# SyncE takes over the wait for the last landings, and GpSimd gets a drain of its own ahead of the four late gathers

## What is computed

```
x = x + concat(y_s5, y_lru) @ w_out
x = x + cross_attend(x, mem_k, mem_v)
gate_w    = softmax(top2(le of the best group)) * pg_sel          # top 2 of 8 experts in the best of 4 groups
combine   = sum_k one_hot(expert_id[k], 32) * gate_w[k]
act       = silu(hf @ w_gate[e]) * (hf @ w_up[e])
out       = sum_e (act * combine[e]) @ w_down[e]
y_prompt, y_sample = rmsnorm(x + out, g_final)
```

## Time and profile before

| | us |
|---|---|
| median of three runs | 1136.78 (1136.31 to 1136.99) |
| the profiled execution | 1137.67 |
| its span | 1135.9 |
| PE busy | 1079.8 |
| DVE busy | 697.8 |
| ACT busy | 277.6 |
| POOL busy (221 instructions) | 191.3 |

### The profile page before, as it was taken

One profiled execution on the slowest core, in us unless ns is written; L12 is line 12 of the kernel. 1 busy time (PEld: TensorE's weight loads), 2 busy tenths in 40 slices (PEclk: granted clock), 3 DMA queues, 4 the chain that ended last, 5 costly groups with the idle time before them and its releaser, 6 DMA issues.

```text
span 1135.9 us, 15543 instructions
## 1 busy us (share of the span) xinstructions
PE 1079.8 (95%) x6141; PEld 617.8 (54%) x6141; DVE 697.8 (61%) x1352; ACT 277.6 (24%) x570; POOL 191.3 (17%) x221
## 2 busy tenths in 40 slices
PE   6999999999999999999999999999899999999991
PEld 4666766678765444788867645555633333333330
DVE  4576499927866655743266677776643555455455
ACT  5201321256652111100033311111301222222232
POOL 5000010101000000000000000000122454565554
PEclk9999999999999999999999999999799999999996
DMA  9109460178373201400045451015789999999951
GB/s 300 42 1 211 41 42 1 45 214 290 122 306 116 65 1 55 168 1 1 1 185 199 172 183 65 32 56 204 284 285 378 412 411 413 414 415 411 411 199 66
DMA packets 75244, 204.97 MB, mean 180 GB/s; under 512 B 25480, under 2 KB 34336, under 8 KB 66816
## 3 DMA queue, kind: packets, MB, share of 16 engines
q1 hardware_dynamic: 54336, 168.82, 42.3%
q0 software_dynamic: 20704, 35.09, 9.1%
q10 hardware_dynamic: 128, 0.03, 0.0%
HBM read 195.23 MB, written 52.18 MB: 218 GB/s over the span
## 4 chain that ended last, share of the span: by engine, by line
PE 80%; DMA 8%; DVE 5%; issue 4%; POOL 1%; ACT 1%; ACTq 0%; POOLq 0%; DVEq 0%
PE bank L800 16%; PE bank L963 9%; PE bank L1333 9%; PE bank L1028 8%; PE bank L1158 6%; PE bank L772 5%; DMA work_firsts<-arena,slots_in 5%; PE bank L1351 4%; PE bank L922 3%; PE bank L1060 2%; PE bank L1125 2%; DMA arena<-work_rows,slots_in 2%; DMA arena<-work_firsts,ptmp 2%; PE bank L889 2%; PE bank L1321 1%
## 5 line engine op out<-in xcount | busy, mean ns | idle before, releaser
L800 PE MATMUL bank<-arena 128*128 128x360 f32 (+1 forms) x576 | 179.8, 473 | 1.0 <-DVE arena L1765 0.9
L1333 PE MATMUL bank<-arena 128*32 128x512 f32 x1536 | 171.9, 599 | 0.8 <-DVE arena L2495 0.8
L800 PEld LDWEIGHTS bank<-arena 128*128 128x128 f32 x576 | 109.6, 192 | 65.9 <-issue 3.5
L2084 DVE TENSOR_TENSOR arena<-arena,bank 128x512 f32<-128x512 f32 (+3 forms) x56 | 68.4, 1221 | 66.0 <-PE bank L1028 37.4
L1333 PEld LDWEIGHTS bank<-arena 128*32 128x32 f32 x1536 | 47.7, 111 | 106.8 <-issue 105.6
L963 PE MATMUL bank<-arena 128*128 128x272 f32 x448 | 103.0, 392 | 0.0
L1158 PE MATMUL bank<-arena 128*128 128x512 f32 x224 | 100.6, 598 | 1.0 <-DVE arena L2249 1.0
L1028 PE MATMUL bank<-arena 128*128 128x512 f32 x224 | 97.7, 593 | 0.0
L963 PEld LDWEIGHTS bank<-arena 128*128 128x128 f32 x448 | 85.0, 190 | 17.4
L1435 ACT ACTIVATE arena<-bank 128x272 f32<-128x272 f32 (+5 forms) x92 | 41.0, 447 | 193.2 <-PE bank L800 130.4
L1351 PE MATMUL bank<-arena 128*32 128x512 f32 x768 | 86.8, 592 | 0.0
(11 more groups left out here) (447 smaller groups left out, 1473.9 us busy)
## 6 DMA issues: line engine op xcount, KB each, us to landing
arena<-in_w_gate SPq DMA_DIRECT2D x32, 1024.0 KB, 10.6
arena<-in_w_up SPq DMA_DIRECT2D x32, 1024.0 KB, 12.5
arena<-in_w_down SPq DMA_DIRECT2D x32, 1024.0 KB, 17.9
arena<-in_ck SPq DMA_DIRECT2D x8, 1024.0 KB, 7.4
arena<-in_cv SPq DMA_DIRECT2D x8, 1024.0 KB, 6.0
arena<-in_w_in SPq DMA_DIRECT2D x3, 2048.0 KB, 14.3
work_firsts<-in_x SPq DMA_DIRECT2D x1, 4352.0 KB
arena<-in_x SPq DMA_DIRECT2D x8, 512.0 KB, 5.8
```

The source lines that it names most:

```text
L800: last = nc.tensor.matmul(b[:, 0:w], win[slot][:, k, m * P:m * P + P], ht[:, k, c0:c0 + w], start=k == 0, stop=k == KD - 1)
L1333: last = nc.tensor.matmul(bank[2 + j % 2][t0:t0 + QT, :].rearrange("p (h n) -> p h n", h=2), xgt[j % 2][:, k, t0:t0 + QT], gu[e % GUB][:, ...
L2084: V.tensor_tensor(out, out, bank[banks(n)][:, :].unsqueeze(1).to_broadcast([P, width, 512]), ADD).then_inc(sem["md_free"], 1)
```

## The change

Three edits. On SyncE, behind all of its loads, eight waits are added: the three `y_st` and the five `o_st`, with the same counts as `landed()` has. On GpSimd, in step 21, one `nc.gpsimd.drain()` is added between the root of tile 18 and the wait ahead of the four late gathers. In the `Else` branch, `landed()` is taken out. The library's DRAIN at the end stays.

```diff
@@ block.sync, at its end
+            for b in range(YSB):
+                sp.wait_ge(sem[f"y_st{b}"], 16 * (NR // YSB - 1))
+            for b in range(YGB):
+                sp.wait_ge(sem[f"o_st{b}"], 32 * len(range(b, NR, YGB)))
@@ step(j), block.gpsimd
                 if j == LATE + 1:
                     main_root(j - 3)
+                    nc.gpsimd.drain()
                     pool.wait_ge(sem["gu_full"], LATE + 1)
                     for c in range(LATE, NR):
                         main_first(c)
@@ block.gpsimd, the end
             with pool.Else():
                 ending()
-                landed()
```

## The result

Twenty runs of each kernel: 1138.39 us median after (1137.29 to 1140.06), 1136.49 before (1135.39 to 1138.05). The ratio is 1.0016, with a 95% interval of 1.001 to 1.0022. The change costs 1.9 us; the forecast was a gain of 2.9.

The account below looks back on a forecast made before the run. GpSimd's final DRAIN and the late-gather chain bound the kernel; DRAIN off the path -4.0, waits and branch -0.3, behind the landing +0.1, late gathers +1.3 total -2.9 us: median 1136.78 to 1133.9, range 1132.5 to 1137.0.

Parts of the forecast that it names:

- What bounds the kernel: At the end GpSimd's DRAIN of 3995 ns; further up, whatever moves the last late gather moves the end.
- The waits on SyncE: At SyncE's end: cost 0, as nothing is queued behind them but its DRAIN of 7 ns.
- Taking out `landed()`: At GpSimd's end: the DRAIN can start near 1129.7 instead of 1131.7, a gain of 2.0 us at unchanged length.
- How long a DRAIN takes: Both GpSimd DRAINs: bookkeeping by packet share, 3.5 us added, 0.5 us last; bounds 0.17 and 4.0 us for each.
- if only the most recent entries are held: GpSimd's queue: the added DRAIN then takes up to 4.0 us and the last one still a small part.
- The added DRAIN on the path: Ahead of the late gathers: it ends at 1099.5 and makes them 1.3 us late, bounds 0 and 3.1.
- the edge: Late gathers: any added DRAIN that ends before about 1101 us costs the same 1.3 us.
- The cover: Added DRAIN: 0.9 us covered by tile 20's store; the first gather ends at 1102.72 with VectorE's second long instruction.
- The last DRAIN: At the block's end: starts about 1131.0, 0.5 us of work beside the last landing, span's end at 1132.9 to 1133.0.
- The fixed price: Both DRAINs: one price of 4.0 us once any DMA was issued; -0.7 us, or up to +1.6; chance 0.20.
- It starts its work only after everything has landed: Added DRAIN: starts near 1097.4, last gather 1.9 us late, -2.3 us; chance 0.15 shared with partial hold.
- The slower rival: Added DRAIN: VectorE holds it off, late gathers +4.3 us; total +0.1 to +2.8; chance of slower 0.07.

Follow-up runs that it names:

- the one with the quiet DRAIN: Changed kernel, with GpSimd also waiting for VectorE's scaling of tile 18 ahead of the added DRAIN; one run, 1141.88 us.
- the change's half alone: The changed kernel without the added DRAIN (SyncE waits, no `landed()` on GpSimd): 1135.08 us against 1136.91 before, ratio 0.998.

## Why the prediction was wrong, step by step

**What bounds the kernel: right.** The end is GpSimd's DRAIN, and the last late gather is on the path. Its delay reached the last scatter whole: from VectorE's add it is 20.88 us in before and 20.92 after.

**The waits on SyncE: right.** They cost nothing. SyncE's DRAIN is at 1134.8, GpSimd's ends at 1135.3.

**Taking out `landed()`: right.** Forecast 2.0 us for a DRAIN of unchanged length; alone it measured 1.8.

**"How long a DRAIN takes": wrong, and this is the step that failed.** I had two lengths, 0.17 us with nothing behind it and 4.0 with everything, and drew a line: 87.5% of the packets, so 3.5 us, and with 4.0 as the upper bound. The work is a price per entry, as supposed, but per entry that is still held. The 4.0 us of before are only 48 entries, because the queue had let 73 go at the 148th of 155 DMAs. At step 21 it holds 103, and the same work costs 8.65 us. The upper bound of 4.0 assumed that at the end there is the most to go over, which is false here. That the share was counted in packets did no harm: by DMAs it is 137 / 155 = 88%. The lower bound was misread, too: the record of 173 ns at the program's start begins before four memsets are done, and a DRAIN with nothing behind it takes 34. I had named the case "if only the most recent entries are held", but bounded it by the last DRAIN again.

**The added DRAIN on the path: followed from that.** With an end at 1102.31, beyond the 1101 us that the prediction had named as the edge, the first gather did not fall into VectorE's second long instruction any more. It started 9.59 us behind the root instead of 1.78, 7.8 late. It then met no long instruction: 1.10 and 1.00 us instead of 2.71 and 1.96, which gives 2.6 back. The last gather's descriptors are 5.2 late and VectorE's add 5.5. The cover that I had counted on was real but worth 2.6 us; it did not hold the delay at 1.3.

**The last DRAIN: the sign right, the size off.** Forecast 0.5 us beside the landing and an end 0.1 behind it. It has 18 entries at 83 ns, 1.5 us, and ends at 1135.28, 0.76 behind the landing as SyncE saw it (1134.52). With work in hand for 1.5 us and 1.7 until the landing, it should have ended sooner. In the changed kernel and in the one with the quiet DRAIN it is 2.44 us from the last descriptors in both. The DRAINs behind the 43rd and the 94th DMA show the same, 1.5 and 3.1 us behind the queue's last packet. So the work is not always hidden beside a landing, as it was with the change's half alone. What a DRAIN does about an entry that has not landed when it gets there was not tried, and these 0.6 us are open.

**The rivals.** The fixed price fell (1.52 us against 4.0). "It starts its work only after everything has landed" fell with the change's half alone. The slower rival, that VectorE holds the DRAIN off, gave the late gathers +4.3, near the 5.5 that came, but for a reason that is false: 8.65 us with VectorE idle. The prediction had given a slower kernel a chance of 0.07. The mechanism that decided was in none of them: that a DRAIN in the middle can cost more than the one at the end.

## What to carry to other kernels

In these kernels a DRAIN on GpSimd goes over the entries that its DMA queue holds there, landed or not, and it also waits for what is in flight; a length measured at one place is no bound for another. Before one is moved or added, count the DMAs since the last DRAIN and where the queue gets full, and ask who waits for GpSimd meanwhile. If a semaphore has told of every landing already, the cheapest DRAIN is none: that was worth 3 to 5 us here, more than any place that was tried for it.

## What the runs showed of the hardware that I had not expected

- GpSimd's DRAIN takes 34 ns with nothing behind it and 82 to 85 ns more for each DMA held, from 6 to 113 of them, whether they landed just now or 100 us ago, whether they had 2 packets on an engine or 14, and whether VectorE is busy or idle.
- The held entries drop by 71 between the 147th DMA and the 149th (9.31 to 3.51 us), and GpSimd starts the 148th about 1.8 us later for it (idle 3.67 us ahead of it instead of 1.83).
- A DRAIN 300 us from the end, in idle time, made the kernel 6.0 us slower: with 112 DMAs behind it the drop did not come before the end, and the last DRAIN was 5.2 us longer.
- In the main loop a DRAIN took 17.1 us: the queue's last packet moved until 14.0 us after the last put's descriptors, and the DRAIN ended 3.1 us behind that.
